# Sampled attention: whole cache pages, keys and values in one transfer, split over two DMA queues by page number

## The reference

```
n_sel = 256                                   # of 2048 cached keys + 4 new ones
sc  = index_scores(q_idx, w_idx, kidx_all)    # which keys each new token reads
sel = top_k(sc, n_sel)
k_sel = cache_k[layer, phys(sel), off(sel)]   # phys: through the page table
v_sel = cache_v[layer, phys(sel), off(sel)]
s = q . k_sel / 8 + rel_bias[rel_bucket(dist)];  p = softmax(s);  o = p . v_sel
```

## Time and profile before

| | |
|---|---|
| median of 3 runs | 3604.21 us (3603.23 to 3606.51) |
| profiled execution | 3601.65 us, span 3600.0 us |
| mean granted TensorE clock | 0.892 |
| PE busy | 3128.0 us (87%) |
| DVE busy | 1962.3 us (55%) |
| ACT busy | 1033.4 us (29%) |
| POOL busy | 142.3 us (4%) |
| DMA issues of cache pages, POOL | 128 of 128.0 KB |
| DMA issues of cache pages, SP | 128 of 128.0 KB |

### The profile page before, as it was taken

How to read it: one execution, slowest core, us unless ns; L and a number is a source line. 1 busy time by engine, 2 the same in 40 slices (tenths; PEclk the granted TensorE clock), 3 DMA queues, 4 the chain that set the end, 5 groups by cost and what they waited for, 6 DMA issues and landing times. The chain is left out here.

```text
span 3600.0 us, 52742 instructions
## 1 busy us (share of the span) xinstructions
PE 3128.0 (87%) x21474; PEld 2842.3 (79%) x21474; DVE 1962.3 (55%) x3262; ACT 1033.4 (29%) x1199; POOL 142.3 (4%) x268
## 2 busy tenths in 40 slices
PE   3999749999833776768799999999999999999996
PEld 3999637878621332358799999999999999999996
DVE  3444266666463885224699888744444444444444
ACT  2222211111121110122344433333334443333332
POOL 0000000000013001300000000000000000000000
PEclk7999759889855555879899999999999999999998
DMA  3444200000015003542444444444545664444441
GB/s 116 155 160 151 84 6 10 19 14 16 13 52 175 24 0 106 171 140 77 162 162 168 156 160 162 167 164 164 166 164 188 206 199 165 162 166 166 166 164 62
DMA packets 115660, 443.70 MB, mean 123 GB/s; under 512 B 24315, under 2 KB 60548, under 8 KB 72052
## 3 DMA queue, kind: packets, MB, share of 16 engines
q1 hardware_dynamic: 101492, 400.85, 33.3%
q0 software_dynamic: 13952, 39.86, 3.6%
HBM read 423.07 MB, written 17.58 MB: 122 GB/s over the span
## 5 line engine op out<-in xcount | busy, mean ns | idle before, releaser
L2021 DVE TENSOR_TENSOR px_w_r<-px_w,px_wh 128x2048 fp32r<-128x2048 f32 x272 | 623.3, 2292 | 725.3 <-ACT px_wh L1857 724.7
L1857 ACT ACTIVATE px_wh<-px_w 128x2048 fp32r<-128x2048 f32 x272 | 521.3, 1917 | 1099.9 <-PE px_bank L255 603.2
L253 PE MATMUL px_bank<-pe_high,px_wh 128*128 128x288 f32 x2304 | 686.6, 298 | 25.8 <-DVE px_w_r L2021 25.8
L254 PE MATMUL px_bank<-pe_low,px_wh 128*128 128x288 f32 x2304 | 680.8, 295 | 0.0
L255 PE MATMUL px_bank<-pe_high,px_w_r 128*128 128x288 f32 x2304 | 678.3, 294 | 0.0
L253 PEld LDWEIGHTS px_bank<-pe_high,px_wh 128*128 128x128 f32 x2304 | 433.0, 188 | 26.2 <-issue 26.2
L255 PEld LDWEIGHTS px_bank<-pe_high,px_w_r 128*128 128x128 f32 x2304 | 434.9, 189 | 0.0
L254 PEld LDWEIGHTS px_bank<-pe_low,px_wh 128*128 128x128 f32 x2304 | 433.7, 188 | 0.0
L253 PE MATMUL px_bank<-px_arena_gh,px_wh 128*128 128x288 f32 x1024 | 303.3, 296 | 1.1 <-ACT px_h L1894 1.1
L253 PE MATMUL px_pair<-px_arena_gh,px_wh 128*128 128x288 f32 x1024 | 303.1, 296 | 0.0
L254 PE MATMUL px_bank<-px_arena_gl,px_wh 128*128 128x288 f32 x1024 | 302.1, 295 | 0.0
(11 more groups left out here) (401 smaller groups left out, 5026.2 us busy)
## 6 DMA issues: line engine op xcount, KB each, us to landing
px_w<-in_peer_u SPq DMA_DIRECT2D x128, 1024.0 KB, 4.9
px_w<-in_peer_v SPq DMA_DIRECT2D x128, 1024.0 KB, 4.8
in_w<-in_w_in SPq DMA_DIRECT2D x49, 1024.0 KB, 4.8
out_w<-in_w_o SPq DMA_DIRECT2D x16, 1024.0 KB, 4.9
px_w<-in_peer_wq SPq DMA_DIRECT2D x16, 1024.0 KB, 4.8
pq_pages<-in_kv_pages POOLq DMA_DIRECT2D x96, 128.0 KB, 3.1
pq_pages<-in_kv_pages SPq DMA_DIRECT2D x96, 128.0 KB, 2.9
g_rest<-px_rest POOLq DMA_DIRECT2D x36, 256.0 KB, 2.6
```

The costliest lines, as they stand in the source:

```text
L253: pe.matmul(out, w_high, high, start=start, stop=False, skip_group_check=True)
L254: pe.matmul(out, w_high, low, start=False, stop=False, skip_group_check=True)
L1857: act.activation(w_high[t % 2][:], w[t % SL][:], ACT.Copy).then_inc(raised, 1)
L2021: v.tensor_tensor(w_low[t % SL][:], w[t % SL][:], w_high[t % 2][:], ALU.subtract) \
```

## The change

Each page comes in one DMA of 256 KB, keys and values together. SP loads the even pages of every sequence, POOL the odd ones, each 8 DMAs per sequence. Both queues wait for `s_summed` before they refill a buffer, since a transfer now writes over the values too. On PE the wait for the values, which stood before `values(i)`, is gone; `scores(i)` waits for all pages of both queues. Eight semaphores stay eight.

```diff
--- before.py
+++ after.py
@@ -1320,7 +1320,7 @@
             cx.sem(f"pp_{x}") for x in ("staged", "scored", "maxed", "exped", "normed", "turned", "moved", "summed",
                                         "mixed", "link", "inverted", "picked"))
         masked = cx.sem("pp_masked")
-        keys_in, values_in = ([cx.sem(f"as_{x}{k}") for k in range(4)] for x in ("keys", "values"))
+        pages_in = [[cx.sem(f"as_pages{q}{k}") for k in range(4)] for q in range(2)]
         s_staged, s_scored, s_maxed, s_exped, s_turned, s_moved_a, s_moved_v, s_summed, s_normed, s_returned, s_mixed = (
             cx.sem(f"as_{x}") for x in ("staged", "scored", "maxed", "exped", "turned", "moved_a", "moved_v", "summed",
                                         "normed", "returned", "mixed"))
@@ -1336,18 +1336,14 @@
         GROUPS = 5
 
         with nc.Block() as block:
-            def load_half(eng, half, sems):
-                source = a["kv_pages"][:, :, half]
+            def load_pages(eng, q):
                 for b in range(B):
                     if b == 2:
                         eng.wait_ge(mixed, NCH)
                     if b >= 4:
-                        if half.start:
-                            eng.wait_ge(s_summed, (b - 4) // 2 + 1)
-                        else:
-                            eng.wait_ge(s_scored, (b - 4) // 2 + 1)
-                    for j in range(PAGES):
-                        load_page(eng, table, source, b, j, pages[b % 4][:, j, half], sems[b % 4])
+                        eng.wait_ge(s_summed, (b - 4) // 2 + 1)
+                    for j in range(q, PAGES, 2):
+                        load_page(eng, table, a["kv_pages"], b, j, pages[b % 4][:, j], pages_in[q][b % 4])
 
             @block.sync
             def _(sp):
@@ -1358,11 +1354,11 @@
                     base = bias_rows[:, TP - t0 - m:]
                     src = bass.AP(base.tensor, base.offset, [[1, m], [2 * TP, 16], [1, TP]])
                     sp.dma_start(bias[t][0:m], src).then_inc(loaded, 16)
-                load_half(sp, slice(0, 2), keys_in)
+                load_pages(sp, 0)
 
             @block.gpsimd
             def _(pool):
-                load_half(pool, slice(2, 4), values_in)
+                load_pages(pool, 1)
 
             @block.vector
             def _(v):
@@ -1592,7 +1588,8 @@
                         pe.wait_ge(s_exped, i)
                     for e in range(2):
                         k = (2 * i + e) % 4
-                        pe.wait_ge(keys_in[k], 16 * PAGES * ((2 * i + e) // 4 + 1))
+                        for q in range(2):
+                            pe.wait_ge(pages_in[q][k], 16 * PAGES // 2 * ((2 * i + e) // 4 + 1))
                     for c in range(GROUPS):
                         j = c * PER
                         w = PER * PAGE if c < PAGES // PER else NEW
@@ -1631,9 +1628,6 @@
                         mm.then_inc(s_turned, 1)
 
                 def values(i):
-                    for e in range(2):
-                        k = (2 * i + e) % 4
-                        pe.wait_ge(values_in[k], 16 * PAGES * ((2 * i + e) // 4 + 1))
                     pe.wait_ge(s_moved_a, 3 * i + 3)
                     pe.wait_ge(s_moved_v, 2 * i + 2)
                     if i:
```

## The result

The changed kernel takes 3624.0 us (median of 5 runs, 3622.3 to 3626.5), the kernel before 3604.4 us in the same comparison: a ratio of 1.0054, 95% interval 1.0039 to 1.0069. That is 19.6 us slower; the forecast was 8 us slower, with a range that ended at 3620 us. The profiled execution took 3622.32 us, 20.7 more than the one of before.

What follows compares the result with a forecast made beforehand. The issue pitch of page loads was taken as the bound. Terms -11.2, +11.0, +12.6, -3.55, -2.5, +0.5 and +0.3 gave 7.1 us, with 1 for the prompt +8 us: 3612 us, range 3605 to 3620.

Steps and rivals of the forecast that it cites:

- The mechanism: Page loads: the first pair's wait goes, gaining 11.2 us; later refills wait for `s_summed`, with PE waits of about 18 us.
- no halving: Rival on page issues: a 256 KB issue takes twice the pitch, +50 us, 3654 us; chance 0.04.
- faster: Rival on refills: so short that pair 1's gain outlives two serial refills, 3597 us or less; chance 0.06.
- One sign that I had named for being wrong: Before the first product: a prompt part starting over 3 us later than now would show the forecast wrong.
- The prompt part's start: Bias table load beside POOL's first pages: 0.4 MB more goes ahead, a delay of 1 us, bounds 0 and 3.
- How long a refill takes, L: Page loads of a pair, from the event freeing the buffers to the last landing: 24 us, ends 21.3 and 26.2.
- `scores(1)` 14.0 us: Pair 1 on PE: right behind the transposes, clock rising about 1 us in, 14.0 us, bounds 13.1 and 15.8.
- `scores(3)` like `scores(2)`, 16.3: Pair 3 on PE: after 18 us of idling it takes 16.3 us, in place of 15.75.
- The rate of 400 GB/s: DMA rate in a refill: the middle between 368 and 434 GB/s, giving 21.0 us of moving.
- memory gives less: Rival on refills: 26 us or more each, from a DMA rate of 368 GB/s, +12.4 us, 3616.6 us; chance 0.15.
- The bound of 358 GB/s: HBM loads by the skill's page: about 358 GB/s for one core, a refill of about 26.6 us, 3617.4 us.

Runs made afterwards that it cites:

- e1: The kernel before, with the keys of sequences 4 to 7 waiting for `s_summed` too: 3656.3 us in one run.
- e2: The changed kernel, with each page as two 128 KB transfers, keys then values, from the same queue: 3662.6 us.
- e5: Sequences 0 to 3 in whole pages as in the changed kernel, sequences 4 to 7 loaded as in the kernel before: 3597.1 us.
- e3: The changed kernel, with POOL waiting for the bias table before its first pages: 3614.2 us.
- e4: The kernel before, with POOL waiting for the bias table before its first pages: 3600.9 us.
- e8: The changed kernel, with only pages 0 to 7 of sequences 4 to 7 loaded: 3606.3 us.
- e9: The changed kernel, with the pages of sequences 4 and 5 swapped with those of 6 and 7: 3622.7 us.
- e10: The changed kernel, with sequences 4 to 7 loaded by SP alone: 3647.7 us.
- e7: As e6, with POOL also waiting for the bias table before its first pages: 3572.9 us, 0.9913 of the kernel before.
- e6: Changed kernel's whole pages for sequences 0 to 3; for 4 to 7 all keys, then all values, over both queues: 0.9938 of the kernel before.

## Why the prediction was wrong

**The mechanism was right.** The wait before `scores(1)` went; both queues idle until `s_summed`; the waits grew before `scores(2)` and `scores(3)`, though to 21.2 and 20.1 us in place of 18; `values(3)` waits no more; a rate near 400 GB/s. e1, e2 and e5 show the parts one by one. The sign of the result was right as well, with the rivals "no halving" and "faster" refuted by POOL's 17.5 us for 16 pages. One sign that I had named for being wrong did come: the prompt part starts over 3 us later.

**The step that failed is the sizes in the sum.** Four terms were too small, together 11.2 us:

- "The prompt part's start", taken as 1 us (bounds 0 and 3): 3.7 us (1160.69 to 1164.42). I let POOL's bytes take room at 368 GB/s and counted only an extra 0.4 MB. But POOL had issued all 16 whole pages by 1148.68 us, some 15 us before the table was there, so all of the extra 1.1 MB could go ahead of it: my upper bound, 3 us, was the likely value. e3 and e4 show the term itself: without POOL beside it the table is there 10.8 and 5.8 us sooner. Four more traces with whole pages first (e5, e8, e9, e10) have it at 1165.3 to 1167.4 us. Miss 2.7 us.
- "How long a refill takes, L", taken as 24 us (ends 21.3 and 26.2): 27.0 us (1449.00 to 1475.99) and 25.8 us (1499.58 to 1525.36). The rate of 400 GB/s, a middle between two unlike transfers, was by luck right for the steady part, but I let it hold from the first byte: 264 and 341 GB/s in the 8 us from 1452 on cost about 2 us, and pair 2 was slower throughout [e8]. I had seen that L counts twice. Miss 3.0 + 1.8 us; the first is outside my upper end.
- "`scores(1)` 14.0 us", "the clock rises about 1 us into it": 15.5 us (1425.88 to 1441.36). Miss 1.5 us. The same stage behind the same transposes took 13.4 us in e5 and 13.2 in e10, so this one is chance as much as error.
- "`scores(3)` like `scores(2)`, 16.3": 18.5 us (1525.36 to 1543.88). The window at 1532 still shows a granted clock of 0.50, 7 us into busy work, and the next one, at 1537, shows 1.00. Miss 2.2 us. This term had no bound of its own in my range, which is a fault: `scores(3)` behind its DMA wait takes from 15.7 us (the kernel before) to 21.2 us (e8) in the traces here. `values(3)` adds 0.5 us and `scores(2)` takes 0.3 back.

8.1 + 2.7 + 4.8 + 1.5 + 2.2 + 0.5 - 0.3 = 19.5 us. The top of the range stood for about +16.3 us in the same terms. The 3.2 us beyond it are 2.2 of `scores(3)` and 0.2 of the small terms, which had no bound, 0.7 of the prompt part and 0.4 of L, less 0.3 that `scores(1)` stayed under its bound. So L is the largest miss of the forecast, and the clock of `scores(3)` the largest reason for leaving the range. All four missed in the same direction, but no common cause is shown. (For 368 GB/s my L should read 26.0 us, not 26.2.)

The rival "memory gives less", L from 26 on and 3616.6 us, described the refills best: L was 26.4 on average. Its reason was another: not 368 GB/s throughout, but the slow first microseconds and pair 2's rate.

**The bound of 358 GB/s** from HBM (the Trainium skill, "DMA: Bandwidth & Descriptors", section "Where 436 GB/s comes from") gave an estimate of 26.6 us for L and 3617.4 us, nearer than my own sum. The trace disagrees with its reason: the refills move 389 to 401 GB/s once under way, and most of the time is lost at the start.

## What to carry to other kernels

When two transfers are merged, the merged one inherits the later of the two waits; here keys that could be fetched a pair ahead had to wait for the values' buffer. The 10 us gained in the first pair were lost nearly three times over, in two refills that take 14.0 and 14.4 us longer than the gaps before; with the old transfers the wait alone costs 52 us (e1). Merge where both halves are free at the same time (the first four sequences) and keep them apart where they aren't (e7, 3572.9 us). And look at what a faster queue pushes aside: the bias table on the other queue was on the critical path, and one wait ahead of the pages was worth 10 us with whole pages (e3, and e7 against e6), though only 3 in the kernel before (e4).

## What the runs showed of the hardware

- POOL and SP together on whole pages start slowly: 264 GB/s at a share of 1.02 in the 3 us from 1452 on, 341 in the next 5, then 389 to 401. SP alone moves 243 GB/s soon after its first issue, at a share of 0.74. A full DMA share is no sign of a full rate.
- A refill of pair 2 is slower than that of pair 3, 27.0 to 27.6 us against 25.8, in three kernels and with other pages.
- A bulk load on one queue delays a load on the other: the 4.7 MB bias table on SP's queue was there at 1164.4 us beside 256 KB pages from POOL, at 1160.7 beside 128 KB ones, and at 1153.6 and 1154.9 with none (e3, e4).
- After an idle stretch PE's granted clock stayed at 0.50 for between some 5 us of work and over 13 us (e8, window at 1517), so the equal work of `scores(3)` took from 15.7 us (the kernel before) to 21.2 us (e8). The length of the idle doesn't order them: 32 us in e10 gave 15.9, 20 in the changed kernel 18.5, 9 in e8 21.2. What sets which of these it will be, the rows don't show.
